# A hybrid decoder layer on one core: 1/rms applied to the finished projections instead of to x, and the loads of x's rows placed later

## The reference, cut to what matters

```python
h = rmsnorm(x, norm_g)                  # x * 1/rms(x) per token * norm_g per feature
z = h @ w_in                            # 2048 x 6144
q_a, k_a, v_a, g_a, u_p, g_p, q_m, g_m = split(z)
y_a = moba_attention(q_a, k_a, v_a) * silu(g_a)      # 8 causal heads of 128
y_p = multiscale_pool(u_p, ...) * silu(g_p)          # window means, a 128x128 map per group
mk, mv = split(rmsnorm(mem, mem_norm_g) @ w_mem_kv)
y_m = memory_attention(q_m, mk, mv) * silu(g_m)      # 4 heads over the 256 memory tokens
out = rmsnorm(x + concat(y_a, y_p, y_m) @ w_out, final_norm_g)
```

## Time and profile before

| | us |
|---|---|
| median of 3 runs | 453.67 (453.28 to 453.78) |
| the profiled execution | 454.34 |
| its span, first to last instruction | 452.2 |
| PE busy in the span | 434.1 (96%) |
| DVE, ACT, POOL busy | 261.6, 219.0, 26.5 |
| mean granted TensorE clock | 0.986 of full speed |

### The profile page before, as it was taken

The page is one execution under the profiler, slowest core; times in us unless marked ns, Lnnn a source line. Parts: engine busy times, 40 slices in busy tenths (PEclk is TensorE's granted clock), DMA queues, the critical chain, the costliest instruction groups (busy, mean ns, idle before and its releaser), DMA issues.

```text
span 452.2 us, 5982 instructions
## 1 busy us (share of the span) xinstructions
PE 434.1 (96%) x2246; PEld 370.9 (82%) x2246; DVE 261.6 (58%) x284; ACT 219.0 (48%) x296; POOL 26.5 (6%) x48
## 2 busy tenths in 40 slices
PE   6986999999999999999999999999999999999992
PEld 6775888888888888888888888888888888888882
DVE  3665497545454548746637575947566384648622
ACT  5575365474343434553555454356464444447311
POOL 1000000000000002000002020002000110211100
PEclk9999799999999999999999999999999999999997
DMA  8999355955555565454436956375635256565022
GB/s 291 414 403 403 140 188 186 372 187 186 186 186 187 185 187 188 130 195 139 147 133 226 414 158 222 107 234 177 209 118 186 96 183 229 183 192 187 1 93 93
DMA packets 25801, 89.76 MB, mean 198 GB/s; under 512 B 2993, under 2 KB 3249, under 8 KB 24881
## 3 DMA queue, kind: packets, MB, share of 16 engines
q1 hardware_dynamic: 24768, 83.90, 54.4%
q10 hardware_dynamic: 1008, 5.52, 3.0%
HBM read 87.31 MB, written 2.10 MB: 198 GB/s over the span
## 4 chain that ended last, share of the span: by engine, by line
PE 89%; DMA 3%; issue 3%; SPq 2%; DVE 1%; ACT 1%; POOL 0%; POOLq 0%; DVEq 0%; ACTq 0%
PE ps L340 34%; PE ps L342 17%; PE ps L355 11%; PE ps L356 11%; PE ps L357 11%; DMA w_raw<-in_w_mem_kv 3%; PE ps L372 1%; PE ps L403 1%; PE ps L399 1%; PE ps L367 1%; SPq L246 1%; PE ps L387 1%; SPq L248 1%; DVE w_lo L663 1%; ACT w_hi L490 0%
## 5 line engine op out<-in xcount | busy, mean ns | idle before, releaser
L663 DVE TENSOR_TENSOR w_lo<-w_raw,w_hi 128x1024 fp32r<-128x1024 f32 x139 | 177.1, 1282 | 139.8 <-ACT w_hi L490 139.1
L340 PE MATMUL ps<-xT,w_hi 128*128 128x512 f32 x640 | 226.7, 399 | 0.0
L490 ACT ACTIVATE w_hi<-w_raw 128x1024 fp32r<-128x1024 f32 x139 | 146.4, 1058 | 155.4 <-PE ps L342 87.1
L342 PE MATMUL ps<-xT,w_lo 128*128 128x256 f32 x640 | 179.2, 280 | 0.0
L340 PEld LDWEIGHTS ps<-xT,w_hi 128*128 128x128 f32 x640 | 120.2, 188 | 29.0
L342 PEld LDWEIGHTS ps<-xT,w_lo 128*128 128x128 f32 x640 | 120.8, 189 | 0.2
L357 PE MATMUL ps<-w_hi,yT 128*128 128x512 f32 x112 | 43.6, 389 | 0.0
L356 PE MATMUL ps<-w_lo,yT 128*128 128x512 f32 x112 | 43.6, 389 | 0.0
L355 PE MATMUL ps<-w_hi,yT 128*128 128x512 f32 x112 | 43.6, 389 | 0.0
L340 PE MATMUL ps<-memT,w_hi 128*128 128x512 f32 x64 | 25.4, 434 | 5.1 <-DVE w_lo L673 2.7
L355 PE MATMUL ps<-w_hi,xT 128*128 128x512 f32 x64 | 25.5, 398 | 0.0
(11 more groups left out here) (122 smaller groups left out, 365.6 us busy)
## 6 DMA issues: line engine op xcount, KB each, us to landing
w_raw<-in_w_in SPq DMA_DIRECT2D x96, 512.0 KB, 4.2
w_raw<-in_w_out SPq DMA_DIRECT2D x32, 512.0 KB, 4.2
w_raw<-in_w_mem_kv SPq DMA_DIRECT2D x15, 512.0 KB, 13.2
rows<-in_x SPq DMA_DIRECT2D x2, 1024.0 KB, 11.7
x_t_raw<-in_x_t SPq DMA_DIRECT2D x8, 256.0 KB, 13.2
rows<-in_mem ACTq DMA_DIRECT2D x2, 1024.0 KB, 8.0
x_res<-in_x ACTq DMA_DIRECT2D x2, 1024.0 KB, 8.0
mem_t_raw<-in_mem_t SPq DMA_DIRECT2D x7, 256.0 KB, 8.1
```

What stands on the lines that cost most here:

```text
L340: pe.matmul(acc, hi[:, t, f * P:(f + 1) * P], moving[:, kt], start=(kt == 0), stop=(kt == KT - 1), skip_group_check=True)
L342: m = pe.matmul(acc[:, 0:S], lo[:, t, f * P:(f + 1) * P], moving[:, kt, 0], start=False, stop=(kt == KT - 1), skip_group_check=True)
L490: act.activation(halves_of(n)[0], w_raw[:, n % RAW], ACT.Copy).then_inc(hi_done, 1)
L663: dve.tensor_tensor(lo, w_raw[:, n % RAW], hi.bitcast(F32), ALU.subtract).then_inc(lo_done, 1)
```

## The change

It does five things.

1. x is split without its norm. `scale_x` is gone, ACT's split of x waits for the transfer alone, and `evacuate` multiplies the result of each of Q0, Q1, K0, K1, GA0, GA1, U, GP, QM and GM by `x_rstd` in one more DVE instruction (behind a wait for its own result, `settle`); V0 and V1 are scaled by 1/rms per token in two instructions in place of one copy.
2. The two loads of x's rows leave SP's queue and are issued from ACT in step 8. ACT squares them in the steps 16 to 19, DVE takes the mean in step 20 (`X_MEAN`), and PE's spread stands behind piece 22 (`X_SPREAD`) and no longer behind piece 9.
3. Memory's gain columns are put ahead of memory in one DRAM tensor and come in the first transfer (`mem_raw`). The other columns (`cols`) come on SP's queue behind MK's last piece, and are waited for in step 10.
4. The first PE work of each group with features on rows has its four hi matmuls first and then its four lo matmuls; in piece 0 PE starts the hi ones when `first_hi` is there, and waits for `first_lo` only behind them.
5. `keep_warm` runs ten matmuls, not seven.

```diff
-SQUARE_STEPS = {5: (0,), 6: (1,), 7: (2,), 8: (3,), 24: (4,), 25: (5,), 26: (6,), 27: (7,)}
+SQUARE_STEPS = {16: (0,), 17: (1,), 18: (2,), 19: (3,), 24: (4,), 25: (5,), 26: (6,), 27: (7,)}
+X_MEAN, X_SPREAD = 20, 22
...
-            sp.dma_start(mem_t_raw[:, 0], mem_t[:, 0]).then_inc(mem_first_landed, 16)
+            sp.dma_start(mem_raw[:, 0:KT + S], mem_head[:, 0:KT + S]).then_inc(mem_first_landed, 16)
...
-                if a in (4, 5):
-                    sp.dma_start(rows[:, a - 4], x_dram[a - 4]).then_inc(rows_landed[a - 4], 16)
+            sp.dma_start(cols[:, :], columns).then_inc(cols_landed, 16)
...
-                        m = pe.matmul(acc[:, 0:S], lo[:, t, f * P:(f + 1) * P], moving[:, kt, 0],
-                                      start=False, stop=(kt == KT - 1), skip_group_check=True)
+                        if kt:
+                            m = pe.matmul(acc[:, 0:S], lo[:, t, f * P:(f + 1) * P], moving[:, kt, 0],
+                                          start=False, stop=(kt == KT - 1), skip_group_check=True)
+                    if n == 0 and t == 0:
+                        pe.wait_ge(first_lo, 1)
+                    if kt == 0:
+                        for f in range(NF):
+                            pe.matmul(ps[:, bank0(g) + f, 0:S], lo[:, t, f * P:(f + 1) * P], moving[:, kt, 0],
+                                      start=False, stop=False, skip_group_check=True)
...
-            keep_warm(7)
+            keep_warm(10)
...
-                    pe.wait_ge(first_lo, 1)
+                    pe.wait_ge(first_hi, 1)
...
-                if g == MV and a == 1:
+                if n == X_SPREAD:
                     pe.wait_ge(diag_ready, 1)
                     spread_rstd(7)
...
-                act.wait_ge(scaled, b + 1)
+                act.wait_ge(x_landed[b], 16)
...
-            act.wait_ge(cols_landed, 16)
             mem_to_hi((0,))
...
+                if n == PPG:
+                    for h in range(TH):
+                        act.dma_start(rows[:, h], x_dram[h]).then_inc(rows_landed[h], 16)
+                if n == X_FIRST:
+                    act.wait_ge(cols_landed, 16)
...
-            def scale_x(b):
-                dve.wait_ge(x_landed[b], 16)
-                own = x_t_raw[:, 2 * b:2 * b + 2]
-                dve.tensor_tensor(own, own, x_rstd[:, :, :].to_broadcast([P, 2, S]), ALU.mult).then_inc(scaled, 1)
...
-                    dve.tensor_copy(dst, ps[:, bank0(g):bank0(g) + TH, :]).then_inc(evacuated, 1)
+                    for h in range(TH):
+                        m = dve.tensor_scalar(dst[:, h], ps[:, bank0(g) + h, :], rstd_in[:, 0, h:h + 1], None, ALU.mult)
+                    m.then_inc(evacuated, 1)
...
+                if g != MK:
+                    settle(m)
+                    m = dve.tensor_tensor(dst[:, :, :], dst[:, :, :], x_rstd[:, :, :].to_broadcast([P, NF, S]), ALU.mult)
+                m.then_inc(evacuated, 1)
```

More of the change, by code:

```diff
@@ L58, with build @@
 BRANCHES = (V1, GA0, GP, GM)
-SQUARE_STEPS = {5: (0,), 6: (1,), 7: (2,), 8: (3,), 24: (4,), 25: (5,), 26: (6,), 27: (7,)}
+SQUARE_STEPS = {16: (0,), 17: (1,), 18: (2,), 19: (3,), 24: (4,), 25: (5,), 26: (6,), 27: (7,)}
 X_FIRST = PPG + 2
-MEM_GAIN, X_GAIN, POOL_SCALE = 0, KT, 2 * KT
+X_GAIN, POOL_SCALE = 0, KT
+X_MEAN, X_SPREAD = 20, 22
 GATES = (GA0, GA1, GP, GM)
-def build(nc, x, mem, x_t, mem_t, columns, w_in, w_mem_kv, w_pool, w_out, final_g, out):
+def build(nc, x, mem, x_t, mem_head, columns, w_in, w_mem_kv, w_pool, w_out, final_g, out):
     with ExitStack() as ctx:
@@ L83, in build @@
         early = ExitStack()
-        mem_t_raw = sb("mem_t_raw", [P, KT, S], F32, early)
+        mem_raw = sb("mem_raw", [P, KT + KT * S], F32, early)
         x_t_raw = sb("x_t_raw", [P, KT, S], F32, early)
@@ L87, in build @@
         yT = sb("yT", [P, KT, 2, S], F32R)
+        sb("past_yT", [P, KT])
         early = ExitStack()
@@ L130, in build @@
         mem_rstd = sb("mem_rstd", [P, 1, M])
-        cols = sb("cols", [P, 2 * KT + NF])
+        cols = sb("cols", [P, KT + NF])
         wp = sb("wp", [P, NF, P])
@@ L217, in build, with mem_t @@
         out_dram = out[0].rearrange("(h p) d -> h p d", p=P)
+        def mem_t(kt):
+            return mem_raw[:, KT + kt * S:KT + (kt + 1) * S]
         def bank0(g):
@@ L514, in mem_to_hi @@
                         act.wait_ge(mem_landed[kt // TPP], 16)
-                    act.activation(memT[:, kt, 0], mem_t_raw[:, kt], ACT.Copy,
-                                   scale=cols[:, MEM_GAIN + kt:MEM_GAIN + kt + 1]).then_inc(mem_hi, 1)
+                    act.activation(memT[:, kt, 0], mem_t(kt), ACT.Copy,
+                                   scale=mem_raw[:, kt:kt + 1]).then_inc(mem_hi, 1)
             def x_to_hi(b):
-                act.wait_ge(scaled, b + 1)
+                act.wait_ge(x_landed[b], 16)
                 for kt in (2 * b, 2 * b + 1):
@@ L721, in evacuate @@
                 hi_part = ps[:, bank0(g):bank0(g) + NF, 0:S]
-                dve.scalar_tensor_tensor(out=dst[:, :, :], in0=hi_part, scalar=FACTOR.get(g, 1.0), in1=part_b[:, :, :],
-                                         op0=ALU.mult, op1=ALU.add).then_inc(evacuated, 1)
+                m = dve.scalar_tensor_tensor(out=dst[:, :, :], in0=hi_part, scalar=FACTOR.get(g, 1.0),
+                                             in1=part_b[:, :, :], op0=ALU.mult, op1=ALU.add)
+                if g != MK:
+                    settle(m)
+                    m = dve.tensor_tensor(dst[:, :, :], dst[:, :, :], x_rstd[:, :, :].to_broadcast([P, NF, S]), ALU.mult)
+                m.then_inc(evacuated, 1)
             def mask_and_max(g, pair):
@@ L775, in _ @@
             dve.wait_ge(consts_ready, 3)
-            dve.wait_ge(cols_landed, 16)
             mem_to_lo((0,))
@@ L791, in _ @@
                     mem_to_lo((2 * a + 4, 2 * a + 5))
-                if n == X_FIRST:
+                if n == X_SPREAD:
                     dve.wait_ge(spread, 1)
@@ L801, in _ @@
                     split_lo(m)
+                if n == X_FIRST:
+                    dve.wait_ge(cols_landed, 16)
                 if X_FIRST <= n < X_FIRST + PPG:
                     x_to_lo(n - X_FIRST)
-                if n == X_FIRST - 1:
+                if n == X_MEAN:
                     mean_square(0)
@@ L884 @@
         "x_t": turned(inputs["x"]),
-        "mem_t": turned(inputs["mem"]),
-        "columns": _np.concatenate([column(inputs["mem_norm_g"]), column(inputs["norm_g"]),
-                                    column(inputs["pool_scale"])], axis=1),
+        "mem_head": _np.concatenate([column(inputs["mem_norm_g"]), turned(inputs["mem"]).reshape(P, KT * M)], axis=1),
+        "columns": _np.concatenate([column(inputs["norm_g"]), column(inputs["pool_scale"])], axis=1),
         "w_in": pieces(inputs["w_in"]),
```

14 lines of the change are left out of this document (5 added, 9 removed).

## The result

The changed kernel takes 445.7 us (median of 4 runs, 444.83 to 446.11), the one before in the same series 453.73 (4 runs, 453.28 to 454.3): a ratio of 0.982, 95% interval 0.9802 to 0.9838. It is 8.0 us faster, where 10.6 were forecast. The profiled execution took 445.7 as well, with a span of 443.7; against the 454.34 and 452.2 of before that is 8.6 and 8.5. The forecast of 443.0 took the whole 10.6 off the median before; but before's profiled execution stood 0.6 above its median and the changed kernel's stands on its own, so 0.6 of the 2.7 us by which 443.0 was missed lies in no stage.

The account below looks back on a forecast made before the run. PE, busy 96%, bounds the kernel, its waits all in the first 46 us. MK -4.8, MV -7.4, Q0 +0.5 and QM's multiplication +1.1 sum to -10.6: 453.67 becomes 443.0 us, 8-in-10 range 440.6 to 445.9.

Parts of the forecast that it names:

- the clock is lost in the opening: Rival, 12%: PE idles from 8.6 to 10.95, then MK runs at half clock for 5.6 us: +2.8, 445.8 us.
- a second stretch at clock 0.50: Sign in the profile after: a second stretch at the lower clock would make the prediction wrong.
- no low clock after 13: Sign expected in the profile after: the granted clock is not low anywhere after 13 us.
- MK, -4.8: Opening and MK: earlier start and no pauses, so MK ends at 30.5 and not 35.3, -4.8 us.
- the start of piece 1: MK: piece 1 starts at 10.95 either way, since its weights land as before.
- Pauses of 1.0 and 1.4 us cost nothing, one of 4.0 did; 2.3 lies between: Opening: reasoning of the 12% rival on whether PE's idle time before piece 1 costs the clock, +2.8 us.
- The rule of the clock: Opening: sustained activity from any source releases the throttled clock; by it MK's term is -4.9 us.
- So no pause is left: MK: weights arrive early and ACT (2.1 us) and DVE (2.5) need less than 2.77 a piece, so no pauses.
- MV, -7.4: MV: without the spread, its 4.0 us pause and low clock, 21.8 us in place of 29.2, -7.4.
- Q0, +0.5: Q0: the spread moves here without a wait, and PE pays only its four passes, +0.5 us.
- The multiplications: Ten DVE products: nine hidden, QM's delays PE before the scores in GM, +1.1 us.
- The paces: Rival, 20% for a microsecond or more: groups switch between 0.347 and 0.353 us a pair; four faster save 1.7, 441.3.

Follow-up runs that it names:

- e7_fill_order: Changed kernel plus nine filling matmuls between pieces 0 and 1, and memory's halves of piece 3 ahead of piece 4's weight split on ACT and DVE: 444.02 us.
- e1_fill: Changed kernel plus twelve matmuls on ones, into a bank nobody reads, between piece 0 and piece 1: 444.98 us.
- e5_qm_in_scores: Changed kernel without QM's multiplication; the maximum and exponential of the memory scores take each token's factor: 443.81 us.
- e6_interleaved_groups: Changed kernel with hi and lo matmuls by turns again in every group but MK: 444.97 us.
- e9_not_deferred: Kernel before, norm not deferred, with x's rows behind MK's last piece in SP's queue and x's split, mean and spread later (spread behind piece 11): 447.64 us.
- e3_rows_in_sp: Changed kernel with x's rows back in SP's queue behind MK's pieces 4 and 5; squares, mean and spread stay late: 448.09 us.
- e12_not_deferred_spread12: As e10_not_deferred_open, with the spread behind piece 12 and x's split one step later: 442.93 us.
- e8_all: Changed kernel with e7_fill_order's opening and e5_qm_in_scores' factors together: 442.63 us.
- e2_align: Changed kernel with the gain columns padded to 256 B, so memory's parts start on 256 B boundaries: 445.02 us.
- e4_rows_sp_spread9: As e3_rows_in_sp, with the squares, mean and spread also back in their old steps (spread behind piece 9): 454.52 us.
- e10_not_deferred_open: e9_not_deferred plus the changed kernel's opening, nine filling matmuls and memory's halves of piece 3 ahead of piece 4's split: 444.05 us.

## Why the prediction was right, and where it was not

445.7 lies inside the range, but close to its upper end and 2.7 above the number. The steps that carry the gain are the forecast ones, with one term at half its size. The number is all but the 445.8 of the rival *the clock is lost in the opening*; that is chance, since the half clock cost half of what that rival gives it. And of the signs that the prediction named as proof against itself one came: a second stretch at clock 0.50, from 12.4 on, where it had said "no low clock after 13".

- **MK, -4.8 forecast, -2.46 measured.** This is the term that was mis-sized, and the rival *the clock is lost in the opening* (12%) happened. Of the 2.3 us, 1.3 are the half clock (1.4, of which I had taken 0.1). 0.35 is the start of piece 1, at 11.29 and not 10.95, mostly because its weights landed later although next to nothing was put ahead of them (8 KB of gains; I had written 18): between kernels with the same queue ahead of them ACT's split of them starts anywhere from 8.26 to 8.83. 0.4 is the pace, 19.86 us for pieces 1 to 7 in e7_fill_order (10.94 to MV's first matmul at 30.80), where I took QM's 0.347 a pair and had 19.4. And 0.2 is the time from PE's end to ACT's next step, which the sum left out. The rival's own price, 2.8, was twice what it cost: the slow matmuls filled 3.2 us, not 5.6.
- **"Pauses of 1.0 and 1.4 us cost nothing, one of 4.0 did; 2.3 lies between".** This was the right question, with too small a chance given to it. PE's idle time was 2.43 us, and e1_fill, which fills it, has no half clock. It may not come every time: of the four executions of the changed kernel three have a mean granted clock of 0.991, the profiled one among them, and one has 0.997 and took 444.83 us. That one has no trace, so where it kept its clock isn't shown.
- **The rule of the clock.** The Trainium skill (TensorE: Matmul & The Clock Gate, Part 1) says that the throttled state is the default and that activity releases it. The rows agree, and matmuls on ones count as activity: with ten warming matmuls PE is at full clock at 7.6, with seven at 9.1, after real work from 5.15. Its other side, that the sooner piece 0 is done, the longer PE stands idle ahead of piece 1, stood only among the rivals; the sum took nothing for it.
- **"So no pause is left" in MK.** Wrong as reasoned, though the changed kernel shows none. I had compared rates (2.1 us of ACT in a piece of 2.77) and not the order of ACT's list, where one late transfer holds up halves that had landed. The slow clock hid it; e1_fill shows 0.48 us, and e7_fill_order takes it away.
- **MV, -7.4 and -6.8.** The 4.0 us pause, the spread and the low clock behind it went as forecast, and nothing was late next. The rest is a pace: eight pieces at 2.80 (22.40) and not at V0's 2.72 from the earlier trace rows.
- **Q0, +0.5 and +0.4.** The spread ran in Q0 without a wait. x's rows, 9.5 us in their transfer, were there in time: ACT squared them from 59.04. I had called a piece of weights 1.05 MB there; it is 0.52 MB, which at one per 2.8 us is 187 GB/s and not 375.
- **The multiplications.** Nine of ten cost nothing, as argued. QM's made the one wait in GM, 0.89 us, less than 1.1; but GM became 1.5 longer, with 0.2 of it in the slower pace of its pieces 1 to 4 and most of the rest right around the wait. e5_qm_in_scores gives nearly all of it back (30.95, and 30.85 before).
- **The paces.** They did change, though by less than the 1.7 us of the rival: K1 and GA1 went to the faster one (-0.40 and -0.41), GM to the slower in four of its pieces (+0.2). What decides between them stays open. The three traces with pairs throughout (before, e6_interleaved_groups, e9_not_deferred) show only that neighbouring plain groups keep the pace they have.

## What to carry to other kernels

Look at the order in each engine's list before you move a transfer: a small operation whose data is there, behind a large one whose data is late, is a pause that no rate shows, and it was found three times here (e1_fill, e3_rows_in_sp, e9_not_deferred). A faster first piece is worth nothing if the second can't start; fill the gap with matmuls, or leave the first piece slow. And take a large edit apart before you credit it: here two moved transfers and a few moved steps alone bring 6.2 us (e9_not_deferred) where the whole change brought 8.0, and with the better opening and one more piece of lead the kernel that keeps the old arithmetic (e12_not_deferred_spread12) is level with the best that defers it (e8_all).

## What the runs showed of the hardware that I had not expected

- The clock fell behind an idle time of 2.43 us (changed kernel), 2.16 (e2_align), 2.19 (e6_interleaved_groups) and 2.38 (e4_rows_sp_spread9); it was low from 12.4 to 15.8, 12.2 to 15.6, 12.1 to 15.5 and 11.2 to 14.6. It stayed up behind 1.55 us (e5_qm_in_scores), 1.70 (e10_not_deferred_open) and all of e3_rows_in_sp's pauses, up to 1.37. When it falls differs: 1.1 us after the work resumed in the first three, 0.2 us after in e4_rows_sp_spread9. In the pause of 4.0 us ahead of the spread it fell 2.9 us into the idle time in the kernel before (at 43.6), and only 0.5 us after its end in e4_rows_sp_spread9 (at 45.4).
- The same pair of matmuls runs at 0.347 or 0.353 us for whole groups, the same 512-column matmul of MV at 0.2267 or 0.2333 (2.72 or 2.80 us for 12), with full granted clock and no wait in both. The two lie 2 to 3% apart, where the whole change brought 1.8%, and no run here steers them.
- Transfers with the same queue ahead of them land up to 0.6 us apart between the traces (ACT's split of piece 1 from 8.26 in e3_rows_in_sp to 8.83), which is as much as several of the edits were expected to show.
